# Second mixer: the first two output products and the last weight splits placed behind all units

## The reference, cut to what matters

```
def diff_mixer(h, w_in, w_out, lam, subln, rel_bias, lambda_init):
    q, k, v = jnp.split(h @ w_in, 3, axis=-1)        # 8 heads, two maps of 64 each, values of 128
    ...
        logits = jnp.einsum('bqhmd,bshmd->bhmqs', qq, k) * scale + bias
        p = masked_softmax(logits, dist >= 0)
        pd = p[:, :, 0] - lam_full * p[:, :, 1]
        o = jnp.einsum('bhqs,bshe->bqhe', pd.astype(v.dtype), v)
        o = rms_norm(o, subln) * (1.0 - lambda_init)
    ...
    return sweep_query_blocks(block, B, S) @ w_out

x = layer_norm(ALPHA * x + (1.0 + g1[:, None, :]) * y, ln_g[l, 0], ln_b[l, 0])
h = modulate(x, sh2, sc2)
y = sq_relu_mlp(h, mlp_w1[l], mlp_w2[l])
```

## Time and profile before

| | |
|---|---|
| median of 3 runs | 1357.98 us (1356.82 to 1367.63) |
| profiled execution, its own time | 1358.01 us |
| its span | 1356.2 us |
| PE busy | 1169.7 us (86%), 7577 matmuls |
| DVE busy | 824.9 us (61%) |
| ACT busy | 615.0 us (45%) |
| POOL busy | 63.9 us (5%) |
| mean granted TensorE clock | 0.919 |

### The profile page before, as it was taken

How to read it: one execution, slowest core, us unless ns; L and a number is a source line. 1 busy time by engine, 2 the same in 40 slices (tenths; PEclk the granted TensorE clock), 3 DMA queues, 4 the chain that set the end, 5 groups by cost and what they waited for, 6 DMA issues and landing times.

```text
span 1356.2 us, 18763 instructions
## 1 busy us (share of the span) xinstructions
PE 1169.7 (86%) x7577; PEld 1026.7 (76%) x7577; DVE 824.9 (61%) x1298; ACT 615.0 (45%) x1097; POOL 63.9 (5%) x93
## 2 busy tenths in 40 slices
PE   2879889899999889766999995995579999699997
PEld 2748756588989779644999994994458887699996
DVE  7576663679898666536756447664665645544444
ACT  0432343554344455634444465365541433655553
POOL 0011144200000000000000000110000000000000
PEclk9989887989999979977999997996688999799999
DMA  9887502259999644311785651440000015355550
GB/s 352 278 295 265 202 1 63 93 188 352 343 353 352 197 156 156 124 62 47 258 284 186 217 187 35 133 147 1 0 1 17 1 63 163 106 187 189 188 178 31
DMA packets 138486, 218.69 MB, mean 161 GB/s; under 512 B 7056, under 2 KB 95504, under 8 KB 138016
## 3 DMA queue, kind: packets, MB, share of 16 engines
q1 hardware_dynamic: 138400, 217.49, 47.5%
HBM read 216.42 MB, written 1.05 MB: 160 GB/s over the span
## 4 chain that ended last, share of the span: by engine, by line
PE 70%; DVE 15%; ACT 7%; DMA 4%; issue 2%; POOL 1%; DVEq 0%; SPq 0%; ACTq 0%
PE bank L468 17%; PE bank L469 16%; PE bank L470 16%; DVE ada_acc L521 3%; DVE low L462 2%; PE bank L2103 2%; ACT high L456 2%; PE bank L2115 2%; DMA ring<-mlp_w 2%; PE bank L2111 2%; PE bank L493 1%; DMA ring<-ada_w 1%; PE bank L2356 1%; DMA ring<-ev_w_in 1%; PE bank L1018 1%
## 5 line engine op out<-in xcount | busy, mean ns | idle before, releaser
L462 DVE TENSOR_TENSOR low<-ring,high 128x2048 fp32r<-128x2048 f32 (+1 forms) x139 | 317.5, 2287 | 272.0 <-ACT high L456 271.6
L456 ACT ACTIVATE high<-ring 128x2048 fp32r<-128x2048 f32 (+1 forms) x139 | 264.3, 1904 | 263.9 <-PE bank L470 175.2
L468 PE MATMUL bank<-act_high,high 128*128 128x256 f32 (+1 forms) x1112 | 326.3, 293 | 15.2 <-DVE act_low L1316 15.2
L469 PE MATMUL bank<-act_low,high 128*128 128x256 f32 (+1 forms) x1112 | 320.7, 288 | 0.0
L470 PE MATMUL bank<-act_high,low 128*128 128x256 f32 (+1 forms) x1112 | 320.5, 288 | 0.0
L468 PE MATMUL bank<-high,act_high 128*128 128x512 f32 (+1 forms) x632 | 234.9, 372 | 15.1 <-DVE ust L1663 10.9
L468 PEld LDWEIGHTS bank<-act_high,high 128*128 128x128 f32 x1112 | 218.7, 197 | 21.8 <-DVE act_low L1316 17.1
L469 PE MATMUL bank<-low,act_high 128*128 128x512 f32 (+1 forms) x632 | 232.3, 368 | 0.0
L470 PE MATMUL bank<-high,act_low 128*128 128x512 f32 (+1 forms) x632 | 232.1, 367 | 0.0
L469 PEld LDWEIGHTS bank<-act_low,high 128*128 128x128 f32 x1112 | 218.8, 197 | 2.7 <-issue 1.7
L470 PEld LDWEIGHTS bank<-act_high,low 128*128 128x128 f32 x1112 | 218.5, 197 | 0.0
(11 more groups left out here) (463 smaller groups left out, 1455.3 us busy)
## 6 DMA issues: line engine op xcount, KB each, us to landing
ring<-mlp_w SPq DMA_DIRECT2D x64, 1024.0 KB, 6.4
ring<-ada_w SPq DMA_DIRECT2D x48, 1024.0 KB, 7.0
ring<-w_up SPq DMA_DIRECT2D x16, 1024.0 KB, 5.5
ring<-w_down SPq DMA_DIRECT2D x16, 1024.0 KB, 5.1
ring<-od_w_in SPq DMA_DIRECT2D x12, 1024.0 KB, 5.2
ring<-w_in SPq DMA_DIRECT2D x11, 1024.0 KB, 5.6
ring<-ev_w_in SPq DMA_DIRECT2D x8, 1024.0 KB, 7.6
ring<-ev_w_out SPq DMA_DIRECT2D x4, 1024.0 KB, 7.9
```

What stands on the lines that cost most here:

```text
L456: e.activation(weights(c)[0], in_ring(("w", c)), ACT.Copy).then_inc(*act.up("high", c))
L462: e.tensor_tensor(low, in_ring(("w", c)), high.bitcast(F32), ALU.subtract).then_inc(*vec.up("low", c))
L468: e.matmul(out_, ah, bh, start=start, stop=False)
L469: e.matmul(out_, ah, bl, start=False, stop=False)
```

## The change

The "out" entries leave `FILLS`. TensorE multiplies pair 0 with `OD_OUT` at the end of step 10 and pair 1 with `OD_OUT + 1` behind step 12, directly ahead of `out_tail`. ScalarE and VectorE split `OD_OUT + 2` at the end of step 9, and `OD_OUT + 3` and `MLP1` behind step 12. No instruction is added or removed. The diff of the TensorE part, with the one of ScalarE (VectorE has the same one with `lower_weights`):

```
@@ FILLS
-                 **{9 + part: ("pair", 3, part) for part in range(3)}, 14: ("out", 0), 18: ("out", 1), 22: ("out", 2)}
+                 **{9 + part: ("pair", 3, part) for part in range(3)}}
@@ diff_tensor
-                elif what[0] == "out" and what[1] < 2:
-                    if what[1] == 0:
-                        out_begin(e, "y1")
-                    e.wait_ge(*vec.at("o2", what[1]))
-                    out_step(e, "y1", OD_OUT + what[1], heads_of(what[1]), what[1] == 0)
+
+            def out_pair(i):
+                e.wait_ge(*vec.at("o2", i))
+                out_step(e, "y1", OD_OUT + i, heads_of(i), i == 0)
...
                     m.then_inc(*pe.up("o2T", i))
+                if step == 10:
+
+                    out_begin(e, "y1")
+                    out_pair(0)
+            out_pair(1)
             e.wait_ge(*vec.at("o2", 2))
             e.wait_ge(*vec.at("o2", 3))
@@ diff_scalar
-                elif what[0] == "out":
-                    round_weights(e, OD_OUT + what[1] + 2)
...
+                if step == 9:
+                    round_weights(e, OD_OUT + 2)
+            round_weights(e, OD_OUT + 3)
+            round_weights(e, MLP1)
```

More of the change, by code:

```diff
@@ L1631, in fill @@
                     lower_weights(e, OD + 3 * what[1] + what[2] + 2)
-                elif what[0] == "out":
-                    lower_weights(e, OD_OUT + what[1] + 2)
             l4 = lam.rearrange("p (a b d) -> p a b d", a=2, b=2)
@@ L1686, in diff_vector @@
                                            oH[grp].bitcast(F32), ALU.mult, ALU.subtract).then_inc(*vec.up("o2", i))
+                if step == 9:
+                    lower_weights(e, OD_OUT + 2)
+            lower_weights(e, OD_OUT + 3)
+            lower_weights(e, MLP1)
         TT_ROWS = (P, P, META)
```

## The result

| | before | changed |
|---|---|---|
| median, runs of one session (4 each) | 1360.35 us (1356.82 to 1367.63) | 1343.36 us (1339.02 to 1350.20) |
| ratio, with its 95% interval | | 0.9875 [0.9838, 0.9912] |
| profiled execution, its own time | 1358.01 us | 1341.99 us |
| from ScalarE's first instruction behind the exponents of head 7 to the first residual ("the stretch") | 581.86 to 624.46: 42.60 us | 582.90 to 608.98: 26.08 us |

The changed kernel is faster by 1.25%. The two profiled executions differ by 16.0 us, and the stretch in which the instructions were moved is 16.5 us shorter.

A forecast was written before the change was run, and what follows sets the result against it. TensorE bounds the kernel, waiting on pair 1's bank behind an unneeded split, then at a second hole, and running slowly after each. First residual from 624.46 to 608.6 saves 15.9 us: 1358.0 - 15.9 = 1342.1; range 1340 to 1348.

The forecast's parts named there:

- Steps 1 to 4: Heads 6 and 7 to pair 2's transposes: `pair_normed` 1 at 584.28, `pair_normed` 2 at 590.08, transposes done at 591.5.
- Steps 5 and 6: Output product on TensorE: pair 0 5.70 us to 597.2, pair 3's transposes 0.60, pair 1 5.70 to 603.5.
- Step 7: The output product's tail: its inputs ready at 602.7, 0.8 us before TensorE wants them, so it starts at 603.5 without a hole.
- Step 8: The first residual follows 21 tail matmuls (4.99 us) at 608.5; VectorE's `MLP1` split and modulation end 608.4; put at 608.6.
- The case given 0.52: TensorE's clock is already high when pair 0's product starts, so it takes 5.70 us; whole time 1342.1 us, chance 0.52.
- the other rule: The Trainium skill's warning: idle gaps between short bursts drop TensorE's clock, so pair 0's product would start at the low clock.
- the second hole: TensorE's 5.60 us idle ahead of pair 3's transposes, behind the split of `MLP1`, and 1.61 more before the tail.
- the second spell of low clock: The tail up to the first residual in the kernel before: 7.12 us from 617.34 to 624.46, against 4.99 at high clock.
- late clock: Rival, second case: the clock rises only inside pair 0's product, 7.80 us for 5.70; 2.6 less gain, 1344.7 us; chance 0.28.
- Slow throughout: Rival: TensorE's clock stays low until the norm, 0.43 us per product for 0.2375; 3 us slower, 1361 us; chance 0.04.
- It gives nothing: Rival: the time saved is waited for again in the MLP, at transfers that don't come earlier; 1358 us; chance 0.06.
- A low stretch later: Rival: 16 us of half-speed clock falls on the moved later stages and costs 8 us; 1350 us; chance 0.10.

The follow-up runs named there:

- one split back: The changed kernel with only the split of `OD_OUT + 2` put back to its earlier place, ahead of pair 1's normalizing: stretch 30.41 us.
- the experiment with the clock kept: The kernel before with 30 matmuls of 512 columns, results unread, put in the idle time ahead of the output product: stretch 40.26 us.
- one split late: The kernel before with only the split of `OD_OUT + 2` moved later, behind the start of pair 1's product: stretch 39.03 us.
- another bank: The kernel before with pair 1's bank passed over when `out_begin` takes its four: stretch 34.04 us, whole 1352.99 us.

## Why the prediction was right

1342.1 us were predicted, 1340 to 1348 as the range; 1343.36 were measured, 1341.99 in the profiled execution, on whose counterpart the sum was made (1358.0 - 15.9; it came to 16.0). That the whole time came so near is in part luck. By their ratios the three sessions give 17.0, 9.6 and 13.6 us, and the interval of the second (5.0 to 14.3) leaves the 15.9 out; medians of the changed kernel lie between 1343.34 and 1346.98. What is borne out closely is the stretch: 42.60 - 26.08 = 16.5 us for 15.9.

- *Steps 1 to 4, the new order.* With 1.04 added, `pair_normed` 1 was due at 585.32 and stands at 585.30; the difference of maps of head 7 at 587.11, found 587.00; transposes of head 7 at 588.01, found 587.90; `pair_normed` 2 at 591.12, found 590.92; its transposes at 591.95, found 591.76. Hand-overs read between two rows of before carry over to another order of the same pieces.
- *`out_begin` asks for nothing new.* Right: L468 at 592.15 stands directly behind the transposes.
- *Steps 5 and 6.* Pair 0 in 5.57 us for 5.70. The mis-sized term is the four transposes: 0.60 was taken from their duration, but the next matmul starts 0.39 and 0.35 us behind their start, since it overlaps with their end. With the 0.2 us of step 4 this makes the tail start at 603.75 where 604.54 was due.
- *Step 7, no hole ahead of the tail.* Right, with `OD_OUT + 3`'s low half ready at 600.88 + 2.29 = 603.17, 0.58 us ahead for the 0.8 named.
- *Step 8, the first residual.* Due at 609.64, found 608.98, since the tail began 0.79 early. That the split of `MLP1` "just fits" held to some tenths: it is now VectorE that holds the residual. The stretch is 26.08 for 26.7.
- *The MLP as long as before, no load late.* Right: 194.95 for 195.23 us, waits for weights 12.8 for 13.4.
- *The clock.* The case given 0.52 came, in all four traces with this order, though not at the same place: the first quick piece stands 3.6, 1.9, 2.4 and 3.2 us ahead of pair 0's product (the changed kernel three times, then with one split back). So it is no narrow escape, but no wide margin either. The row at 550 foretold it: a run of small pieces with no hole brings the clock up. By the other rule it would have cost 2.6; where the rise fell inside the product, in before, it cost 2.2 to 2.3 by the experiment with the clock kept.
- *The kinds of the gain.* Here the prediction was wrong in how it sorted the gain, though not in its sum. "4.3 for the split ahead of pair 1, and the rest for the second hole and for the second spell of low clock" leaves out the largest share. The split is 4.36 us of the 10.95, the other 6.59 are the bank, which comes free only when pair 1, behind its own chain of small pieces, is normalized. The schedule had that, since it put the product where the bank is free already; the sentence that sorted the gain did not. It also sets 7.12 us against 4.99, which leaves out the end of the 21st matmul and the hand-over: at the high clock it is 5.23 (603.75 to 608.98). By the table of stretches the splits are worth 8.5, the bank 6.9 on top of them (8.6 alone), and the products' place 1.1.
- *The range.* Its upper end, 1348, is called the second case with the same slack: 1344.7 with the 1.9 between 1342.1 and 1344 is 1346.6. The four runs reach from 1339.02 to 1350.20, so the range holds for the median and not for every run.
- *Loads.* Four are announced and three named. Behind them in SP's queue stands the load of `gate_rows` (608.69), probably the fourth; the first residual did not wait for it.

Of the rivals, *late clock* did not occur in any trace in which the products stand behind the units: in all four of these, pair 0 ran at the high clock. *Slow throughout* did not occur. *It gives nothing* falls with the stages' lengths. *A low stretch later* is real: it cost 2.5 and 3.7 us in the second block's mixer (332.31 for 329.80, 333.25 for 329.57), not the 8 that were assumed. It comes to before as well, and ahead of the stretch too, 5.9 us in one trace. So it widens the spread of single runs; nothing ties it to the change, but runs enough to exclude a small loss were not made.

## What to carry to other kernels

A matmul that opens an accumulation asks for its banks, and in a rotation that can be the bank of an unrelated piece that is still to be read: look up the bank's last reader before moving the product, for one line that skips the bank gave 8.6 us here by itself, and with the splits moved nearly all that the new order gave. Work that nobody needs yet, such as the split of a later chunk, belongs behind the small pieces on which TensorE waits, not between them; its price is what of it the chain can't hide: 4.36 us where both halves of the split stood on it, 2.41 where squares and root of the next pair (1.71 us) ran on ScalarE beside VectorE's half. Judge such an edit by the length of the stretch it touches: here that repeats within 0.1 us for the changed kernel and 1.1 us for before, while whole runs of one kernel lie up to 18 us apart.

## What the runs showed of the hardware

- The number of slow products after a hole is not fixed. After the same 10.95 us of idle time ten were slow in one trace of before and seven in another, 7.80 and 7.08 us for the same 24. After 6.58 us seven were slow with all splits moved (7.14 us), and after 6.59 us 13 with one split late (8.31 us). The Trainium skill (TensorE: Matmul & The Clock Gate, What's actually happening) says that the number of slow matmuls varies from run to run of one kernel; these traces agree.
- Whether a hole drops the clock is not decided by its length alone. 3.20 us left it high (four transposes in 0.63 us, all splits moved), 3.19 us let it fall to 0.50 (1.09 us, `MLP1` split late), and the holes of 0.82 to 1.48 us in the traces of the changed kernel never did. After 3.99 us ahead of the transposes of head 5, three of them took 0.52 us in the trace with the 30 matmuls and 0.87 in the one with another bank, though both programs are the same up to there.
- Matmuls whose result is thrown away can bring the clock up in a hole of 10.9 us: with thirty of them it was 0.50 from 577 to 579, 1.00 from 580 on, and still 1.00 when the product started, after 2.25 us of idle time. Here that bought 2.3 us; filling the hole with real work buys the hole as well.
- Low stretches with TensorE at work come and go from run to run (mean clock 0.905 in the slowest run of before, 0.920 in the fastest) and go with 18 us of difference in 1360.
